# One stage for the mLSTM and the linear recurrence, a whole head after each token tile

## What is computed

```
def mlstm(q, k, v, i_pre, f_pre):          # 4 heads of 64; k and q are silu(conv(...))
    g = cumsum(log_sigmoid(f_pre)); u = i_pre - g
    m = running max of u
    s = (q @ k.T) / 8 * exp(u[key] - m[query])    for key <= query
    h = (s @ v) / max(abs(s.sum(-1)), exp(-(g + m)))
    return sigmoid(o) * rms_norm(h)

def rwkv7(r, w, k, v, a, b):               # 4 heads, state 64 x 64
    for t in tokens:
        S = S * w[t] + (S @ a[t]) b[t].T + v[t] k[t].T
        y[t] = S @ r[t]
    return (group_norm(y) + bonus) * gate
```

## Time and profile before

| | us |
|---|---|
| median of three runs | 3215.77 (3215.07 to 3219.16) |
| the profiled execution | 3219.56 |
| its span, first to last instruction | 3217.8 |
| PE, PEld, DVE, ACT busy | 3079.1, 2593.0, 1389.7, 1109.9 |
| mean granted clock of TensorE | 0.961 |
| mLSTM of layer 0 | 592.1 to 657.9 |
| linear recurrence of layer 0 | 657.9 to 758.2 |

### The profile page before, as it was taken

How to read it: one execution, slowest core, us unless ns; L and a number is a source line. 1 busy time by engine, 2 the same in 40 slices (tenths; PEclk the granted TensorE clock), 3 DMA queues, 4 the chain that set the end, 5 groups by cost and what they waited for, 6 DMA issues and landing times. The chain is left out here.

```text
span 3217.8 us, 41971 instructions
## 1 busy us (share of the span) xinstructions
PE 3079.1 (96%) x17718; PEld 2593.0 (81%) x17718; DVE 1389.7 (43%) x1909; ACT 1109.9 (34%) x1568; POOL 13.9 (0%) x25
## 2 busy tenths in 40 slices
PE   8999999888999999999999888999999989999998
PEld 7888788677888888888888667888878878888887
DVE  3333445545333254333345546333346157545642
ACT  3322334323222245222334423222235245434431
POOL 0000000000000000000000000000000000000000
PEclk9999999688999999999999878999999989999999
DMA  3333311002133332233411102123342200213322
GB/s 132 99 98 110 124 41 61 17 5 99 40 98 96 108 124 72 92 98 116 137 32 61 33 5 85 35 92 98 111 137 85 66 25 29 65 60 98 98 93 85
DMA packets 71482, 254.48 MB, mean 79 GB/s; under 512 B 8056, under 2 KB 9208, under 8 KB 71296
## 3 DMA queue, kind: packets, MB, share of 16 engines
q1 hardware_dynamic: 71296, 251.81, 24.3%
HBM read 249.68 MB, written 2.10 MB: 78 GB/s over the span
## 5 line engine op out<-in xcount | busy, mean ns | idle before, releaser
L206 PE MATMUL ps<-h_hi,w_space 128*128 128x512 f32 (+3 forms) x5440 | 1515.5, 364 | 17.4 <-DVE h_lo L304 17.2
L206 PEld LDWEIGHTS ps<-h_hi,w_space 128*128 128x128 f32 x5440 | 981.2, 190 | 181.3 <-DVE h_lo L304 20.7
L194 DVE TENSOR_TENSOR w_space<-w_raw,w_space 128x1024 fp32r<-128x1024 f32 x440 | 536.2, 1225 | 1081.1 <-ACT w_space L187 1080.5
L206 PE MATMUL ps<-h_lo,w_space 128*128 128x512 f32 (+3 forms) x2720 | 985.6, 362 | 0.0
L187 ACT CAST w_space<-w_raw 128x1024 fp32r<-128x1024 f32 x440 | 457.8, 1047 | 991.4 <-PE ps L206 591.1
L216 PE MATMUL ps<-w_space 128*128 128x512 f32 x3312 | 769.2, 394 | 16.6 <-DVE w_space L194 15.8
L216 PEld LDWEIGHTS ps<-w_space 128*128 128x128 f32 x3312 | 627.4, 190 | 148.8 <-issue 12.7
L206 PEld LDWEIGHTS ps<-h_lo,w_space 128*128 128x128 f32 x2720 | 516.1, 190 | 78.8 <-issue 1.4
L582 ACT CAST w_space<-act_p 128x512 fp32r<-128x512 f32 x88 | 54.6, 621 | 187.4 <-DVE act_p L594 172.4
L597 DVE TENSOR_TENSOR w_space<-act_p,w_space 128x512 fp32r<-128x512 f32 x88 | 61.0, 693 | 69.8 <-ACT w_space L582 69.8
L594 DVE TENSOR_TENSOR act_p<-act_s,ps 128x512 f32<-128x512 f32 x88 | 60.0, 681 | 71.3 <-PE ps L206 71.3
(11 more groups left out here) (382 smaller groups left out, 2441.7 us busy)
## 6 DMA issues: line engine op xcount, KB each, us to landing
w_raw<-in_w_ffn_in SPq DMA_DIRECT2D x176, 512.0 KB, 3.6
w_raw<-in_w_ffn_out SPq DMA_DIRECT2D x88, 512.0 KB, 3.6
w_raw<-in_w_in SPq DMA_DIRECT2D x64, 512.0 KB, 3.7
w_raw<-in_w_up SPq DMA_DIRECT2D x44, 512.0 KB, 3.6
w_raw<-in_w_out SPq DMA_DIRECT2D x24, 512.0 KB, 3.6
w_raw<-in_w_down SPq DMA_DIRECT2D x22, 512.0 KB, 3.6
w_raw<-in_w_ple_gate SPq DMA_DIRECT2D x16, 512.0 KB, 4.9
gain_pre<-in_gains_pre SPq DMA_DIRECT2D x10, 512.0 KB, 5.1
```

The lines of the kernel that those rows point to most:

```text
L194: nc.vector.tensor_tensor(self.lo(n), self.raw[:, n % SLOTS, :], self.hi(n).bitcast(F32), ALU.subtract).then_inc(self.lo_ready, 1)
L206: m = nc.tensor.matmul(c.ps[:, bank, t], part[:, cols], moving[:, k, t], start=(k == 0 and i == 0), stop=(k == KD - 1 and i == 2))
```

## The change

The two stages become one, `recurrence_stage`, with one barrier and one set of semaphores. Its TensorE loop, by tile, is the loop of the linear recurrence with a head of the mLSTM behind the tile's solve: `spread_max` before it, then four `scores` and `sums`. The other engines get the same: ScalarE the four exponentials, the head's squares, and after every second head a root; VectorE exponents, weighting, normalising.

PSUM is shared, so several things go from many banks to one: one bank of scores (each waits for the weighting of the one before), one of the spread maximum, one of the sums, and the row pairs use the banks of the turned factors. `next_state` waits for `shaped`, the first part of the finish of an earlier tile. The gate is at the start of the stage still, now followed by the turn of `u` into columns. Silu and sigmoid of the mLSTM are on ScalarE between the gate's copies and the copy of the first squaring. The convolved q and k stand in `c.proj` instead of `c.y`; semaphores of the last block are made there. The transposes of the values and the start of the gates' work are at the start of the stage.

In the diff, the loop of TensorE and the waits that it needs:

```diff
-def mlstm_stage(nc, c, l, selectors):
...
-def rwkv_stage(nc, c, l, loras, chunk_masks):
+def recurrence_stage(nc, c, l, selectors, loras, chunk_masks):
...
-        SQ_BANK, T_BANK, AB_BANK, KV_BANK, S_BANK, Y_BANK = 0, 1, 2, 3, 6, 7
-        ROW_BANKS = (4, 5)
+        SQ_BANK, T_BANK, Y_BANK, SCORE_BANK, MAX_BANK, SUM_BANK = 0, 1, 4, 5, 6, 7
+        ROW_BANKS = (2, 3)
...
+                def scores(h, s):
+                    i, p0 = NT * h + s, DH * (h % 2)
+                    if s == 0 and h % 2 == 0:
+                        pe.wait_ge(qk_ready, 2 * (h // 2 + 1))
+                    if i:
+                        pe.wait_ge(weighted, i)
...
-                pe.wait_ge(padded, 1)
+                pe.wait_ge(padded, 2)
                 turn(0)
+                values_by_token()
                 pairs_of_a(0)
...
+                a_values(0)
+                pe.wait_ge(u_ready, 1)
+                columns_of(MAX_BANK, u, u_turned)
+                pe.wait_ge(gate_ready, 2)
                 pairs_of_r(0)
...
+                    if t >= 2:
+                        turn_back(t - 2)
+                    if t == 0:
+                        pe.wait_ge(low_ready, 1)
+                        pe.wait_ge(v_copied, 2)
+                        columns_of(SUM_BANK, low, low_turned)
...
+                    spread_max(h)
                     solve(t)
-                turn_back(NT - 2)
+                    for s in range(NT):
+                        scores(h, s)
+                    sums(h)
                 local(NT - 1)
                 steps_of_state(NT - 1)
+                heads_back(0)
+                turn_back(NT - 2)
                 next_state(NCH - 2)
                 outputs(NT - 1)
+                heads_back(1)
                 turn_back(NT - 1)
...
+                act.wait_ge(u_turned, 1)
+                nc.scalar.copy(u_col[:, :, :], c.ps[:, MAX_BANK, 0:NT * M_HEADS]).then_inc(u_copied, 1)
+                for t in QK_ORDER:
+                    nc.scalar.activation(qk[:, t, :], qk[:, t, :], ACT.Silu).then_inc(qk_ready, 1)
+                for j in range(2):
+                    nc.scalar.activation(o_gate[:, j, :], o_gate[:, j, :], ACT.Sigmoid).then_inc(o_ready, 1)
                 for t in range(NT):
+                    h = t
                     powers(t, 1)
...
+                    for s in range(NT):
+                        weights(h, s)
+                    head_squares(h)
+                    if t % 2:
+                        head_roots(t // 2)
...
-            mlstm_stage(nc, c, l, a["selectors"])
-            rwkv_stage(nc, c, l, a["loras"], a["chunk_masks"])
+            recurrence_stage(nc, c, l, a["selectors"], a["loras"], a["chunk_masks"])
```

More of the change, by code:

```diff
@@ new lines, in columns_of, with spread_max @@
+                def columns_of(bank, rows, done):
+                    for n in range(NT):
+                        m = nc.tensor.matmul(c.ps[:, bank, n * M_HEADS:(n + 1) * M_HEADS], rows[:, n * P:(n + 1) * P],
+                                             c.mats[0:4, MATS.index("ident"), 0:4], start=True, stop=True)
+                    m.then_inc(done, 1)
+                def spread_max(h):
+                    if h == 0:
+                        pe.wait_ge(max_ready, 1)
+                        pe.wait_ge(u_copied, 1)
+                    else:
+                        pe.wait_ge(below_ready, NT * h)
+                    nc.tensor.matmul(c.ps[:, MAX_BANK, :], select[:, h, :], run_max, start=True, stop=True).then_inc(max_spread, 1)
@@ new lines, in scores @@
+                def scores(h, s):
[4 more added lines that the diff above has]
+                        pe.wait_ge(weighted, i)
+                    else:
+                        pe.wait_ge(v_copied, 1)
+                    nc.tensor.matmul(c.ps[:, SCORE_BANK, 0:S - s * P], qk[p0:p0 + DH, 2 + h // 2, s * P:(s + 1) * P],
+                                     qk[p0:p0 + DH, h // 2, s * P:S], start=True, stop=True).then_inc(s_done, 1)
@@ new lines, in sums @@
+                def sums(h):
+                    pe.wait_ge(weighted, NT * (h + 1))
+                    if h == 0:
+                        pe.wait_ge(floored, 1)
+                        pe.wait_ge(v_copied, 2)
+                    else:
+                        pe.wait_ge(hid_ready, h)
+                    for n in range(NT):
+                        for s in range(n + 1):
+                            m = nc.tensor.matmul(c.ps[:, SUM_BANK, n * (DH + 1):(n + 1) * (DH + 1)],
+                                                 weighted_s[:, s, n * P:(n + 1) * P], v_tok[:, s, h, :],
+                                                 start=(s == 0), stop=(s == n))
+                    m.then_inc(nd_done, 1)
@@ L1980, in _ @@
                 ch = Chain(dve, chain_s)
-                ch.mark(nc.vector.memset(state[:, 0, :, :], 0.0))
                 def masks_of_a(t):
```

464 lines of the change are left out of this document (193 added, 271 removed).

## The result

The changed kernel took 3253.01 us (median of four runs, 3246.36 to 3257.20) against 3217.47 for the kernel before beside it: a ratio of 1.0105, 95% interval 1.0081 to 1.0129. It is slower by 35.5 us. The forecast was 3335, slower by 119, with a range from 3240 up. The sign held, and the range held only because its low end had been drawn down to another case (its own case had 3312 to 3358); the slowdown was more than three times too large. The third case, "the tiles win it back" at 3250, is what happened.

The account below looks back on a forecast made before the run. It took TensorE and its clock level as the bound: 19.0 + 5.3 + 118 + 60 + 24 = 226.3 us a layer against 165.8, +60.5, twice +121, giving 3335 us. Own range 3312 to 3358, low end extended to 3240.

Parts of the forecast that it names:

- the tiles win it back: Rival: the clock falls in every head, the tile behind raises it again; 183 us a layer, 3250 us; chance 0.14.
- Nothing behind it looks like the gate's passes: Work after the first squaring: no passes there raise the clock, so 1.2 GHz to the end of the stage.
- the first case: The forecast's own case: lower clock level to the end of each stage, 226.3 us a layer, 3335 us; chance 0.76.
- start to the first squaring: Stage start from 592.1: clears, memsets, transposes, corners, gate and turn of u at the lower level; 19.0 us.
- four tiles, with the extra in tile 0: The linear recurrence's four tiles: 70.7 us becomes 118 at 1.2 GHz, plus 5.3 in tile 0.
- four heads: mLSTM heads between solve and next squaring, whole on PE's path with nothing beside them: 15.3 us each, 14 the first; 60.
- end: Behind the last head: VectorE's row of steps, state, outputs at 1.70 us a head, centre to finish; 24 us, before 16.5.
- the term of 5.3: Tile 0: first power copy delayed 3.4 us by ScalarE's queued activations and table loads, plus 1.9 for the floor row's turn.
- The factor 1.8: Lengthening of PE's busy time in the tiles at the lower clock, taken by the transposes; 65.75 us becomes 118.
- The clock holds: Rival: the clock stays at 2.4 GHz through the heads' pauses; 159 us a layer, 3202 us, faster; chance 0.07.
- the change touches nothing else that takes time: Premise: only the two layers' recurrences, the clock dips at slices 8 to 10 and 23 to 25, matter; layer 0 doubled.

Follow-up runs that it names:

- experiments 11 and 12: The kernel before with 64 extra 64-by-64 passes at 605 us, row halves alternating (11) or held for 32 each (12): 3223.21 and 3237.18 us.
- Experiment 7: The changed kernel with the four silu and two sigmoid activations at the start of ScalarE's list: 3241.91 us, ratio 1.0069.
- experiment 2: The changed kernel with all four heads behind the last tile instead of one behind each: 3245.92 us, ratio 1.0087.
- experiment 1: The changed kernel with the mLSTM heads left out on all engines, leaving the tiles and the start: 3112.02 us.
- experiment 12: The kernel before with 64 extra 64-by-64 passes at 605 us, 32 from the upper rows, then 32 from the lower: 3237.18 us.
- experiment 5: The changed kernel with each head's scores spread between its tile's squarings and inverse steps, sums behind solve: 3236.70 us, ratio 1.0059.
- experiments 14 and 15: 14: changed kernel with heads spread over tiles, outputs step in four, silu and sigmoid first, filling passes: 3186.00 us; 15: the same with further reordering: 3171.93 us.
- experiment 6: The kernel with heads spread over the tiles (3236.7 us), its outputs step cut into four separated parts: 3234.03 us, ratio 1.0046.
- experiments 3 and 13: The changed kernel, 3: with ten filling passes in every head's pauses, 3251.15 us; 13: with tiles 1 to 3's first squaring behind the state steps, 3266.80 us.
- experiment 15: The kernel of 3186.0 us with VectorE's norm first, tile 0's masks and first squaring earlier, PE waiting for the first memset only: 3171.93 us, ratio 0.9848.

## Why the prediction was wrong, step by step

**What bounds the kernel, and which case was right.** PE in order, a whole head on its path with nothing beside it, the clock as the question: all that holds. The mistake is one sentence, "Nothing behind it looks like the gate's passes ... So I take 1.2 GHz to the end of the stage". It counted all small passes as of one kind. The mLSTM's passes that had not raised the clock were of 64 or 4 rows against long streams, or sums; the corners were 48 instructions of 64 by 64, with the row half held. A squaring is 64 by 64 as well, but its passes alternate between the two row halves of the array, and experiments 11 and 12 show that this can decide (its pairing with the output half and a bank differ with it). The tile has five such steps and as many of the inverse in the same form. No row of before had a squaring at the lower level, so the case was not covered by the evidence in either direction; a row that is missing should have cost the first case much of its 0.76.

**The terms, layer 0:**

| term | forecast | measured | where |
|---|---|---|---|
| start to the first squaring | 19.0 | 19.5 | 592.1 to 611.6 |
| four tiles, with the extra in tile 0 | 118 + 5.3 | 81.2 | four stretches without the spreads |
| four heads | 60 | 54.9 | 50.5 and four spreads of 1.1 |
| end | 24 | 23.3 | 747.7 to 771.0 |
| sum | 226.3 | 178.9 | |

The start is right by luck: the first squaring began at 611.6 (forecast 611.1), but by two errors that cancel. The clock was back at 602.1, before the gate, and the gate ended at 605.1 where 607.2 stood; then PE waited 2.5 us for the first masks, a wait that the forecast had not. The prediction had read that transposes and corners do not raise the clock, and the kernel before has 8 transposes there. The changed kernel has 16, and with them and only the first of the corners it came back:

```profile
597.80:602.00 4.20, 4.15 (x26) 3.82 (x28) 0.00 (x0) 2.11 (x4) 0.00 (x0) 0.50 0.00 0
```

In tile 0 the copy of the first power began at 615.6, where 616.3 stood; but the whole tile was 20.0 us, spread included, since the clock was up for most of it. Of the term of 5.3 the trace has a wait of 2.6 for the 3.4 and a turn of 1.15 for the 1.9. Experiment 7 shortened the wait to 0.7 and the stage did not get shorter, since another wait grew by as much.

The tiles are the mis-sized term: 81.2 instead of 123.3, which is 42 of the 47 us by which the stage was missed. The factor 1.8 for the lower level is sound where the level was the lower: squaring 1.97 against 1.15, sums 4.53 against 2.34, outputs 7.1 against 3.8. It just applied to 3 to 9 us behind each head, and to the first 8 us of tile 0, and not to the whole tile. (The prediction's own range has a slip: -10 and +13 a layer about 3335 give 3315 to 3361, not 3312 to 3358.)

The heads were 10.9 for the first (three of its four scores at the upper level) and 13.5, 12.9, 13.2, plus 1.1 of spread. The forecast's 15.3 at the lower level is met by experiment 2, 14.7 to 16.7. No run gives the heads their second bank of scores back, so what the single bank costs in them is not shown. The end at 23.3 was at 0.50 throughout, as put.

**The rivals.** "The clock holds" had 0.07 and a condition that the trace decides: in all four heads it falls, 3 to 5 us behind the first score, among the pauses, like the stretch from 741 in the earlier trace rows. "The tiles win it back" had 183 us a layer against 178.8 measured. Its argument against itself was the earlier trace rows, PE busy 18.94 of 20 us at 0.50. That row is true, and so is its reading that busy time alone doesn't do it; it was wrongly carried over to another kind of work. The rival itself was not right everywhere: in experiment 1 tile 0 had 10 us of unbroken work at 0.50. The Trainium skill, in TensorE: Matmul & The Clock Gate, Part 1, has activity as what releases the throttle. The tiles agree, the mLSTM of before and experiment 12 (6.70 of 6.70 us busy, 0.50) do not, as long as activity is read as busy time.

**The total.** 2 times 12 us from the stages, 24, is what the mechanism gave; in the profiled execution 8.5 more are the stretch behind layer 1. Its dip stands in slice 33 of the earlier trace rows, beside the two that the prediction names, and "the change touches nothing else that takes time" left it out. The case of 3250 was met to 3 us, which is luck: 17 a layer against 12, and the stretch behind layer 1 made up the difference.

## What to carry to other kernels

Before a forecast hangs on a clock that comes back or doesn't, list for each kind of pass in the new order whether the trace has it at either level; a kind without a row is an open case, with a chance near even, not part of its nearest neighbour. A head or any other chain that alternates between engines costs its own length where nothing stands between its pieces, 13 us here. Putting the pieces between the tile's steps was not enough either (174 to 178 us in experiment 5, against 166.7 before); it took the further changes of order in experiments 14 and 15 to make the stage 26 us shorter than before. Compare variants stage by stage before comparing totals: the same code elsewhere varied by 13 us between the profiled executions of these kernels.

## What the runs showed of the hardware

TensorE's return to 2.4 GHz does not follow its busy time. 64 passes of 64 by 64 with alternating row halves brought it back after 3.4 us; the same passes with the row half held for 32 at a time left it at 0.50 for 6.7 us, and three passes of 64 rows and 512 columns left it there for 5.5 us. Both orders ran at the same rate at the lower level (130 instructions in 6.7 us, 65 in 3.4). Other work brought it back too: 16 transposes with a few corners in the changed kernel (at 602.1), the gate's long passes in the kernel before (at 668.8). A squaring is no guarantee: with other passes around it the clock stayed at 0.50 through 10.0 us of unbroken work in experiment 1.

In these stages the clock mostly fell behind short waits. In tiles 1 to 3 of experiments 5 and 6 it fell 0.5 to 1.7 us behind the end of a wait of 2.0 us, and in experiments 3 and 13 in the outputs step of tile 3, behind a wait of 0.8 us. That is no rule: the changed kernel has a wait of 0.8 us ahead of the same step of tile 3 and kept the clock there, and experiment 6 kept it behind a wait of 2.0 us in tile 2. It can also fall while TensorE is busy without a gap: in experiment 15 at 618.3, behind 3.40 of 3.40 us of work, most of it passes of 4 and 64 rows. What share each kind of pass has in a fall or a return is open.
